# Compact norms in a recurrent mixer and differential attention staged between the steps of a projection

## The reference

```python
# recurrent mixer, per head of 64 channels
a = sigmoid(a0 + ad @ a2)
kk = (k * k_k).reshape(B, S, H, 64)
kk = kk / maximum(sqrt(sum(kk * kk, -1)), 1e-12)
k = k * (1 + (a - 1) * k_a)
...                                    # state update over the tokens gives y
y = (y - mean) * rsqrt(var + 64e-5) * ln_w + ln_b      # mean, var per head
bonus = sum(r * k * r_k, -1) * v

# differential attention, 16 heads, d = 64, two softmaxes a head
q, k, v, g = split(h @ w_in, 4)
q = rmsnorm(q, per 64) * d ** -0.5 ; k = rmsnorm(k, per 64)
s = q k^T + bias ; s masked ; p = softmax(s)
attn = p[:, 0] - lam * p[:, 1]
o = rmsnorm(attn @ v, per head of 128) * (1 - lam_init)
y = (o * silu(g)) @ w_out
```

## Time and profile before

| | us |
|---|---|
| median of 3 runs | 1906.8 |
| lowest, highest | 1901.38, 1909.23 |
| profiled execution | 1912.7 |
| its span | 1910.8 |
| TensorE busy | 1760.3 (92%) |
| VectorE busy | 995.6 (52%) |
| ScalarE busy | 749.0 (39%) |
| GpSimd busy | 94.0 (5%) |

### The profile page before, as it was taken

The page is one execution under the profiler, slowest core; times in us unless marked ns, Lnnn a source line. Parts: engine busy times, 40 slices in busy tenths (PEclk is TensorE's granted clock), DMA queues, the critical chain, the costliest instruction groups (busy, mean ns, idle before and its releaser), DMA issues. The chain is left out here.

```text
span 1910.8 us, 31186 instructions
## 1 busy us (share of the span) xinstructions
PE 1760.3 (92%) x13605; PEld 1670.7 (87%) x13605; DVE 995.6 (52%) x1254; ACT 749.0 (39%) x1065; POOL 94.0 (5%) x80
## 2 busy tenths in 40 slices
PE   7969999679999968998999999997799899999899
PEld 6969998579998956988999999964499899999899
DVE  4565353773536426447444444329655755445543
ACT  5532222523223335444333334336445533444432
POOL 2010000300001100003000000000001000000000
PEclk8989999789999978998999999978699999999999
DMA  8632222233224652553656565390065465556453
GB/s 249 181 99 81 85 79 67 56 100 89 78 78 134 186 102 81 185 175 102 184 181 186 181 185 182 106 139 30 13 199 164 121 190 158 150 147 186 143 183 116
DMA packets 252608, 255.57 MB, mean 134 GB/s; under 512 B 8625, under 2 KB 249298, under 8 KB 252024
## 3 DMA queue, kind: packets, MB, share of 16 engines
q1 hardware_dynamic: 251816, 253.37, 46.2%
q0 software_dynamic: 656, 0.21, 0.1%
HBM read 250.86 MB, written 2.69 MB: 133 GB/s over the span
## 5 line engine op out<-in xcount | busy, mean ns | idle before, releaser
L212 DVE TENSOR_TENSOR w_lo<-w_raw,w_hi 128x1024 fp32r<-128x1024 f32 (+1 forms) x452 | 552.0, 1224 | 597.0 <-ACT w_hi L207 596.9
L240 PE MATMUL ps<-xt,w_hi 128*128 128x256 f32 x2736 | 798.8, 292 | 26.9 <-DVE w_lo L212 23.3
L241 PE MATMUL ps<-xt,w_hi 128*128 128x256 f32 x2736 | 780.0, 285 | 0.0
L242 PE MATMUL ps<-xt,w_lo 128*128 128x256 f32 x2736 | 779.7, 285 | 0.0
L207 ACT ACTIVATE w_hi<-w_raw 128x1024 fp32r<-128x1024 f32 (+1 forms) x452 | 471.0, 1046 | 683.6 <-PE ps L242 535.8
L240 PEld LDWEIGHTS ps<-xt,w_hi 128*128 128x128 f32 x2736 | 531.4, 194 | 39.0 <-issue 27.8
L241 PEld LDWEIGHTS ps<-xt,w_hi 128*128 128x128 f32 x2736 | 531.5, 194 | 2.5 <-issue 2.5
L242 PEld LDWEIGHTS ps<-xt,w_lo 128*128 128x128 f32 x2736 | 530.6, 194 | 0.0
L249 PE MATMUL ps<-w_hi,xt 128*128 128x256 f32 x832 | 238.9, 287 | 0.0
L251 PE MATMUL ps<-w_hi,xt 128*128 128x256 f32 x832 | 235.8, 283 | 0.0
L250 PE MATMUL ps<-w_lo,xt 128*128 128x256 f32 x832 | 235.8, 283 | 0.0
(11 more groups left out here) (372 smaller groups left out, 1536.2 us busy)
## 6 DMA issues: line engine op xcount, KB each, us to landing
w_raw<-in_a_w_in SPq DMA_DIRECT2D x128, 512.0 KB, 3.6
w_raw<-in_w_in SPq DMA_DIRECT2D x120, 512.0 KB, 3.6
w_raw<-in_b_w_in SPq DMA_DIRECT2D x96, 512.0 KB, 3.7
w_raw<-in_w_out SPq DMA_DIRECT2D x32, 512.0 KB, 4.6
w_raw<-in_a_w_out SPq DMA_DIRECT2D x32, 512.0 KB, 3.5
w_raw<-in_b_w_out SPq DMA_DIRECT2D x32, 512.0 KB, 3.7
arena<-in_x SPq DMA_DIRECT2D x2, 1024.0 KB, 7.7
w_raw<-in_w_in SPq DMA_DIRECT2D x8, 256.0 KB, 5.8
```

The source lines that it names most:

```text
L212: k.nc.vector.tensor_tensor(k.wl[:, p % RING, :, 0:w], k.raw[:, p % RAW, :, 0:w], k.wh[:, p % RING, :, 0:w].bitcast(F32), ALU.subtract).th ...
L240: pe.matmul(os, h[:, cs], xt[:, kt, 0:S], start=st and ct == 0, stop=False, skip_group_check=True)
L241: pe.matmul(os, h[:, cs], xt[:, kt, S:2 * S], start=False, stop=False, skip_group_check=True)
L242: last = pe.matmul(os, l[:, cs], xt[:, kt, 0:S], start=False, stop=sp, skip_group_check=True)
```

## The change

In the recurrent mixer the norms are kept for 8 heads by 256 tokens (`small`, 8 partitions) instead of being spread over 128 partitions first: the sums go to 8 rows, the root and the reciprocal are taken there, and a product with `chosen` spreads the result into PSUM, from which VectorE multiplies. Both norms of both halves are changed, the one of the finish (L945 to L951) in the same way with its product (vb2) two steps behind the sums, the list of slots is wider, and GpSimd's order changes. The differential attention moves into the second projection: its chunks are ordered queries and keys, values, gate; the norms of queries and keys follow each chunk; each head has seven steps in 24 slots, now with its own root and reciprocal of the output norm; bias tables lie in the place of the gate tiles (ten heads) and in a buffer of their own (six), and are loaded in 16 parts between weight pieces. The output projection of layer one makes its weight halves alternately with the operand, as the third layer does. `diff_attention` and the two blocks go.

```diff
-        for after, gap in ((end(c + 1), 2), (0, 3), (0, 5), (0, 8), (end(c + 2), 4), (end(c + 3), 3),
-                           (end(c + 4), 3), (end(c + 5), 3), (0, 3), (0, 5), (0, 8), (0, 6), (0, 6), (0, 4)):
+        for after, gap in ((end(c + 1), 4), (0, 4), (0, 8), (0, 8), (end(c + 2), 6), (end(c + 3), 4),
+                           (end(c + 4), 4), (end(c + 5), 4), (0, 4), (0, 8), (0, 10), (0, 3), (0, 8), (0, 10), (0, 5)):
             now = max(now + gap, after + 2)
             at.append(now)
+        now += 2
         for _ in range(2 * (12 + 4 * LV)):
             now += 3
             at.append(now)
-        for _ in range(3):
-            now += 5
+        for _ in range(4):
+            now += 6
             at.append(now)
...
+    small, chosen = ar[0:8, 4096:4352], ar[0:8, 4352:4864]
+    eight = view(con[0:8, K_ID:K_ID + 1], [[1, 8], [0, 64]])
+    weighted = ar[:, 5120:6144].rearrange("p (j t) -> p j t", t=S)
...
             if hh:
-                pe.wait_ge(ve, 1)
+                pe.wait_ge(yn, 6)
...
-            for _ in range(7):
+            for _ in range(8):
                 yield
             pe.wait_ge(s2, hh + 1)
-            for q in range(2):
-                mm = pe.matmul(k.ps[:, q, :], blk, bonus(hh)[:, 2 * q:2 * q + 2, :], start=True, stop=True)
+            for u in range(4):
+                mm = half_sums(k, pe, u, 8, k.ps[0:8, 0, 0:S], bonus(hh)[:, u, :], u == 0, u == 3)
             mm.then_inc(ss, 1)
             yield
+            pe.wait_ge(rn, 2 * hh + 2)
+            pe.wait_ge(sl, 2 * hh + 1)
+            for u in range(4):
+                mm = pe.matmul(k.ps[:, u // 2, (u % 2) * S:(u % 2) * S + S], spread(u), small, start=True, stop=True)
+            mm.then_inc(nb, 1)
             yield
             yield
...
             act.wait_ge(ss, hh + 1)
-            nc.scalar.activation(bonus(hh).rearrange("p (q j) t -> p q (j t)", q=2), k.ps[:, 0:2, :],
-                                 ACT.Sqrt).then_inc(nr, 1)
+            nc.scalar.activation(small, k.ps[0:8, 0, 0:S], ACT.Sqrt).then_inc(nr, 1)
+            yield
...
-            n2 = bonus(hh)
             dve.wait_ge(nr, hh + 1)
-            nc.vector.tensor_scalar(n2, n2, 1e-12, None, ALU.max).then_inc(rn, 1)
+            nc.vector.tensor_scalar(small, small, 1e-12, None, ALU.max).then_inc(rn, 1)
             dve.wait_ge(rn, 2 * hh + 1)
-            nc.vector.reciprocal(n2, n2).then_inc(rn, 1)
-            dve.wait_ge(rn, 2 * hh + 2)
-            nc.vector.tensor_tensor(bt(hh), bt(hh), n2, ALU.mult).then_inc(kn, 1)
+            nc.vector.reciprocal(small, small).then_inc(rn, 1)
+            yield
+            dve.wait_ge(nb, hh + 1)
+            nc.vector.tensor_tensor(pair(bt(hh)), pair(bt(hh)), k.ps[:, 0:2, :], ALU.mult).then_inc(kn, 1)
...
             dve.wait_ge(vs, hh + 1)
-            nc.vector.tensor_scalar(em.rearrange("p (q j) t -> p q (j t)", q=2), k.ps[:, 2:4, :], 1.0 / 64, 64e-5,
-                                    ALU.mult, ALU.add).then_inc(ve, 1)
+            nc.vector.tensor_scalar(small, k.ps[0:8, 2, 0:S], 1.0 / 64, 64e-5, ALU.mult, ALU.add).then_inc(ve, 1)
             yield
             dve.wait_ge(vr, hh + 1)
-            nc.vector.reciprocal(em, em).then_inc(yn, 1)
-            dve.wait_ge(yn, 6 * hh + 1)
-            nc.vector.tensor_tensor(pv, pv, em, ALU.mult).then_inc(yn, 1)
+            nc.vector.reciprocal(small, small).then_inc(yn, 1)
+            yield
+            dve.wait_ge(vb2, hh + 1)
+            nc.vector.tensor_tensor(pair(pv), pair(pv), k.ps[:, 0:2, :], ALU.mult).then_inc(yn, 1)
...
+                    nc.gpsimd.tensor_copy(chosen.rearrange("p (a b) -> p a b", a=8), eight).then_inc(sl, 1)
+                    for u in range(4):
+                        j = j0 + u
+                        nc.gpsimd.tensor_scalar(weighted[:, u, :], pr[:, u, :], k.va[:, A_RK + j:A_RK + j + 1], None,
+                                                ALU.mult).then_inc(bo, 1)
                     pool.wait_ge(kr, 4 * hh + 4)
                     pool.wait_ge(ka, 5 * hh + 4)
                     nc.gpsimd.tensor_tensor(pk, pk, spare(hh), ALU.mult).then_inc(ka, 1)
                     pool.wait_ge(ka, 5 * hh + 5)
-                    for u in range(4):
-                        j = j0 + u
-                        nc.gpsimd.tensor_scalar(spare(hh)[:, u, :], pr[:, u, :], k.va[:, A_RK + j:A_RK + j + 1], None,
-                                                ALU.mult).then_inc(bo, 1)
                     pool.wait_ge(bo, 5 * hh + 4)
-                    nc.gpsimd.tensor_tensor(spare(hh), spare(hh), pk, ALU.mult).then_inc(bo, 1)
+                    nc.gpsimd.tensor_tensor(weighted, weighted, pk, ALU.mult).then_inc(bo, 1)
+                    pool.wait_ge(me, hh + 1)
+                    nc.gpsimd.tensor_copy(chosen.rearrange("p (a b) -> p a b", a=8), eight).then_inc(sl, 1)
...
+def second_chunks(wa, tiles, tok):
+    return tiles(wa, 0, T2_Q, 16) + tok(wa, 2 * D, T2_V, 16, 8) + tiles(wa, 3 * D, T2_G, 8)
+
+
+def second_slots(g):
+
+
+    def end(c):
+        return g.starts[PIECES * (c + 1)] if c + 1 < len(g.chunks) else g.slots
+    at = [end(0)]
+    for c in range(8):
+        at += [end(c) + 2, end(c) + 8]
+    at.append(end(7) + 14)
+    for c in range(8, 16):
+        at += [end(c) + 2, end(c) + 8, end(c) + 16]
+    now = end(15) + 14
+    at[-1] = now
+    at.append(now)
+    now += 8
+    for _ in range(8):
+        now += 3
+        at.append(now)
+    for _ in range(DIFF_H + 1):
+        at += [now, now + 4, now + 6, now + 10, now + 13, now + 17, now + 21]
+        now += 24
+    for n in range(8):
+        now = max(now, end(D_G + n) + 2)
+        at.append(now)
+    return at
+
+
+def second_layer(k, a, g1, g2, g3, mix, yg, xtok):
...
+        def spread(pe, n):
+            pe.wait_ge(rcd, n // 8 + 1)
+            pe.wait_ge(ch, 2)
+            if n >= 2:
+                pe.wait_ge(xn, n - 1)
+            for u in range(2):
+                m = 2 * (n % 8) + u
+                mm = pe.matmul(k.ps[:, 2 + n % 2, u * S:(u + 1) * S], chosen[m // 8][:, (m % 8) * P:(m % 8) * P + P],
+                               rnq, start=True, stop=True)
+            mm.then_inc(sp2, 1)
...
+            for i in range(DIFF_H + 1):
+                h = i - 1
+                if i < DIFF_H:
+                    pe.wait_ge(xn, 16)
+                    if i:
+                        pe.wait_ge(pre, i)
+                    for t in range(2):
+                        ps_ = slice(64 * t, 64 * t + 64)
+                        q, key = k.proj[ps_, T2_Q + i, :], k.proj[ps_, T2_K + i, :]
+                        o = k.ps[:, t, :]
+                        pe.matmul(o[:, 0:P], q[:, 0:P], key[:, 0:P], start=True, stop=True)
+                        mm = pe.matmul(o[:, P:3 * P], q[:, P:S], key, start=True, stop=True)
+                    mm.then_inc(sco, 1)
+                yield
+                if i:
+                    pe.wait_ge(att, 2 * h + 2)
+                    for b in range(3):
+                        mm = pe.transpose(k.ps[:, 2, b * P:(b + 1) * P], sc[:, h % 2, 0, b * P:(b + 1) * P], ident)
+                    mm.then_inc(tpd, 1)
+                yield
+                yield
+                if i:
+                    pe.wait_ge(pte, h + 1)
+                    pe.wait_ge(k.evac_a, k.evacs[g2.c0 + D_V + h // 2 + 1][0])
+                    if h:
+                        pe.wait_ge(od, h)
+                    o = k.ps[:, 3, 0:S]
+                    pe.matmul(o, v[:, 0, h * P:(h + 1) * P], pt[:, 0:S], start=True, stop=False)
+                    pe.matmul(o[:, P:S], v[:, 1, h * P:(h + 1) * P], pt[:, S:3 * P], start=False,
+                              stop=True).then_inc(pvd, 1)
+                yield
+                yield
+                if i:
+                    pe.wait_ge(sqo, h + 1)
+                    pe.matmul(k.ps[:, 4, 0:S], one, sqh, start=True, stop=True).then_inc(sso, 1)
+                yield
+                yield
...
+            for i in range(DIFF_H + 1):
+                h = i - 1
+                yield
+                if i:
+                    act.wait_ge(tpd, h + 1)
+                    nc.scalar.activation(pt, k.ps[:, 2, 0:3 * P], ACT.Copy).then_inc(pte, 1)
+                yield
+                if i < DIFF_H:
+                    act.wait_ge(nm2, 2 * i + 2)
+                    for t in range(2):
+                        for tt in range(NT):
+                            nc.scalar.activation(sc[:, i % 2, t, rows[tt]], sc[:, i % 2, t, rows[tt]], ACT.Exp,
+                                                 bias=st[:, i % 2, 0, t, tt:tt + 1],
+                                                 accum_out=st[:, i % 2, 1, t, tt:tt + 1]).then_inc(exd, 1)
+                yield
+                if i:
+                    act.wait_ge(pvd, h + 1)
+                    nc.scalar.activation(sqh, k.ps[:, 3, 0:S], ACT.Square).then_inc(sqo, 1)
+                yield
+                yield
+                if i:
```

(86 more changed lines are left out.)

388 lines of the change are left out of this document (152 added, 236 removed).

## The result

| | before | after |
|---|---|---|
| median, us | 1905.7 (4 runs) | 1855.8 (4 runs) |
| lowest, highest | 1901.4, 1909.2 | 1854.4, 1863.3 |
| profiled execution, its span | 1912.7, 1910.8 | 1854.5, 1852.7 |

The ratio is 0.9747, 95% interval 0.9713 to 0.9781. The changed kernel is faster, by 49.9 us between medians, where 65 was forecast from the profiled execution and 1842 for the median.

What follows compares the result with a forecast made beforehand. TensorE plus its idle holes was taken as the bound. Gains 34 + 3.4 + 28 = 65 us off the profiled 1912.7 give 1847; with the median 5.9 lower, 1842, range 1827 to 1857.

Steps and rivals of the forecast that it cites:

- part 3: Differential attention staged into the second projection: 138.5 us removed, added work and stalls come back, gain 28 us.
- Part 1: Mixer in the first projection: compact norms and wider slot list fill TensorE's idle holes, gain 34 us.
- the second wait of the square sums: Mixer's second half: TensorE's wait at L554 falls from about 18 us (17.8 listed) to about 9.
- the weight wait in front of the one-tile chunk: Mixer's second half: three pieces' lead is worth only 12 slots at the small chunk, costing 3 us.
- rival C: Mixer holes move instead of closing: gain there only 11 to 18 us, total 1858 to 1865; chance 0.17.
- Part 2: Start of layer one's output projection: alternating operand and weight halves cut 7.1 us to 3.7, gain 3.4.
- sums and broadcasts, with switching: Staged attention: 32 sum and 32 broadcast products at 0.43, 27.5 us, plus 3 for switching kinds of matmul.
- products of 16 heads: Staged attention: TensorE's transposes, scores, values and square sum take 2.65 us a head, 42.4 in all.
- loop of VectorE and ScalarE: Staged heads: in-order loop of 13.3 us against TensorE's 11.3, so 2.0 us idle a head, 28 over 14 heads.
- entry: Staged attention's start: first scores wait for the last scaled key, about 1.2, plus second roots; 3 us.
- tail and restart: After the second projection: last evacuation, Silu, product 2.3, boundary 0.4, restart 3.7; 6.4 us.
- rival A: VectorE and ScalarE's loop does not bind in the staged heads: 11.3 us a head, total 1814; chance 0.14.

Runs made afterwards that it cites:

- the first part alone: Kernel before with the mixer's compact norms and wider list of slots, without the other changes: 1876.8 us, ratio 0.9841.
- the later entry: Changed kernel with the first three attention steps in the second projection moved from 0, 2, 8 to 12, 16, 28 slots behind the first chunk: 1849.3 us.
- the short reciprocal: Changed kernel with VectorE's reciprocal of a head's root taken over only 16 of its 256 columns: 1838.2 us, ratio 0.9625.
- the narrow norms alone: Kernel before with the mixer's compact norms but the old tight spacing of steps, attention unstaged: 1894.0 us, ratio 0.9945.
- the wider list alone: Kernel before with the mixer's wider list of slots, norms still 128x1024 wide, attention unstaged: 1890.9 us, ratio 0.9926.

## Why the prediction was right, and which term was off

The direction, the range and the mechanisms held; the time was 13.8 us above the forecast. At 1855.8 it stands only 1.2 us inside the forecast's own range of 1827 to 1857, and that is partly luck: in part 3 two terms were too small by 13.0 us together, and one that came out 4.3 better took some of it back. The parts measured: 31.1 (medians), 3.4 (7.1 - 3.7), 16.9 (stage distance), sum 51.4, against 34, 3.4 and 28.

**Part 1** was forecast at 34. The profiles gave 671.9 - 637.5 = 34.5, but this flatters it. In ten profiles of kernels with this same first layer nsa's first product lies from 636.1 to 641.3, with the first part alone at 641.7, and the profiled execution before was itself 6 us over its median. The median says 31.1. The steps held in outline: the second wait of the square sums, forecast at about 9, was 2.1 (up to 3.6 in other profiles), the transposes' went to under 1, the weight wait in front of the one-tile chunk was 2.5 for 3. Both halves of the argument, shorter chains and wider spacing, were needed, and rival C fell.

**Part 2** held, 3.7 us from operand to first matmul as in the third layer. No run took it by itself.

**Part 3** is the term that was mis-sized: 28 forecast, 16.9 measured. What was added, against what was forecast:

| | forecast | measured |
|---|---|---|
| sums and broadcasts, with switching | 27.5 + 3 | 16 x 1.17 + 16 x 1.24 = 38.6 |
| products of 16 heads | 42.4 | 16 x 2.64 = 42.2 |
| loop of VectorE and ScalarE | 28 | 16 x (12.76 - 11.28) = 23.7 |
| entry | 3 | 6.4 got back by the later entry, 1.5 left (sums 0.7, scores 0.8): 7.9 |
| tail and restart | 6.4 | 6.3 |
| not attributed | | 2.9 |
| sum | 110.3 | 121.6 |

The broadcast step's 1.24 us comes from this timeline of the changed kernel (1.26 from 1070.58 to 1071.84 and 0.22 to the next matmul, less 0.12 each):

```profile
1070.58 0.28 PE L251 MATMUL ps<-w_hi,xt 128*128 128x256 f32 x1
1070.78 1.12 PE L1237 MATMUL ps<-t_sq,proj 32*128 32x256 f32 x4
1071.84 0.38 PE L249 MATMUL ps<-w_hi,xt 128*128 128x256 f32 x1
1072.06 0.28 PE L250 MATMUL ps<-w_lo,xt 128*128 128x256 f32 x1
```

The failed step is first "I take off 3 for switching between kinds of matmul": 32 steps at 0.31 to 0.38 are 11, and the earlier trace rows had not shown it, since the forecast read there only the distance of two small products. Second, "3 for the entry": the forecast had put the first scores there and not the first sums. Square and sums of chunk 0 stand 2 and 8 slots (0.7 and 2.9 us) behind it, while its result waits for the layer's norm:

```profile
852.19 1.75 DVE L1642 RECIPROCAL rs_bc<-rs_bc 128x256 f32<-128x256 f32 x1 [0.58 <-ACT rs_tok L1636]
...
854.00 0.69 DVE L316 TENSOR_TENSOR proj<-ps,rs_bc 128x512 f32<-128x512 f32 x1
...
856.24 0.29 DVE L1357 TENSOR_REDUCE df_ls<-t_sq 128x2 f32<-128x128 f32 x1
```

Only then can ScalarE take its Exp and the square. Third, the loop came out better than forecast. The period of 12.76 us takes in two distances of 11.1 and 11.3, before the loop binds; the twelve behind them have a mean of 13.0 (12.8 in the last five), against 13.3, and TensorE stands 1.4 to 2.2 us at the square sum, against 2.0. The loop was rightly named, and rival A (it does not bind) falls by the short reciprocal. Of the 2.9 us left over, 1.5 are the first head at the clock of 0.85; the rest is open and smaller than what the old order's distance varies by.

The bias transfers cost nothing that shows: in the whole stage neither ScalarE nor TensorE waits for a transfer. No run took them away.

## What to carry to other kernels

When work is laid between the steps of a full TensorE, write down the loop of the other engines per iteration, with every in-order neighbour, and then the buffers: moving an instruction out of the loop helped only once the PSUM bank that it reads was doubled. Price a stage by what it adds between two projection matmuls, not by the length of its products, and group small products of one kind. Read a gain from medians: a distance between two profiles can be off by several microseconds in stages where TensorE often stands. The first step behind a new operand's norm must be placed by that norm's chain, not by the end of the chunk.

## What the runs showed of the hardware

A reciprocal of 256 columns takes 1.74 us on 8 partitions (L874 above), 1.74 on 32 and 1.75 on 128: the compact form saves because there are 256 columns instead of 1024, not because of the 8 partitions.

Changing from the projection's matmuls to a float32 pair and back costs 0.31 us (1.17 us a step, less 0.86 for the pair), and 0.38 where the pair is a broadcast from 32 partitions (1.24 less 0.86); two such broadcasts in one group pay it once (2.11 us).

A switch from the root's table to Exp's took 1.29 us where ScalarE waited for nothing (1087.02 to 1088.31 above), and cost nothing where it waited anyway (period 12.76 us with the switches and without).

The same instructions of nsa, from its first product to the first matmul of the output projection, took from 78.5 to 81.7 us in ten profiles. The granted clock goes with it, 0.85 over the whole stretch in the changed kernel (78.5) and 0.82 with the later entry (81.7). Two stretches at the same distance from nsa's first product, in these two kernels:

```profile
672.92:685.55 12.63, 9.93 (x49) 8.23 (x50) 9.36 (x23) 7.68 (x26) 0.00 (x0) 0.87 0.01 1
685.55:700.55 15.00, 15.00 (x90) 11.83 (x89) 13.84 (x40) 9.61 (x34) 0.00 (x0) 1.00 0.00 1
```

```profile
676.30:689.00 12.70, 9.88 (x41) 7.62 (x42) 9.41 (x23) 7.68 (x26) 0.00 (x0) 0.77 0.01 1
689.00:704.00 15.00, 15.00 (x78) 12.21 (x78) 11.29 (x32) 7.67 (x27) 0.00 (x0) 0.87 0.00 1
```

So 3 us between two profiles, in a stage that a change does not touch, may be no more than this; nsa gave 3.2 between the profiles before and after. The old attention stage varied more, here from the end of the second projection to the first matmul of the third, with the narrow norms alone and with the wider list alone, which leave that stage as it was:

```profile
1226.85:1362.13 135.28, 103.29 (x434) 68.25 (x433) 86.42 (x198) 66.34 (x190) 2.80 (x3) 0.79 0.39 60
```

```profile
1216.90:1358.47 141.57, 109.64 (x433) 71.43 (x433) 86.43 (x198) 66.13 (x190) 2.80 (x3) 0.74 0.39 57
```

VectorE's work is the same, the clock 0.79 and 0.74, and 6.3 us lie between them.
